# Reading the moving activations of a two-block transformer kernel from the last column to the first

## What is computed

```python
proj = rmsnorm(h, norm1_w) @ w_in
h = h + mixed @ w_out
z = rmsnorm(h, norm2_w) @ mlp_w1
h = h + jnp.square(jax.nn.relu(z)) @ mlp_w2
...
proj = x @ w_in_2
merged = g_a * (o_a @ w_o_dsa) + g_b * (o_b @ w_o_moba)
y = merged @ w_out_2
y = (jax.nn.silu(g) * u) @ w_ffn_out
```

## Time and profile before

| | before |
|---|---|
| median of 3 runs | 2574.3 us |
| span of the profiled execution | 2573.8 us |
| PE busy | 2555.9 us (99%), 15948 matmuls |
| PEld busy (loads of the stationary side) | 2297.6 us (89%) |
| DVE busy | 1572.9 us (61%) |
| ACT busy | 1189.7 us (46%) |
| POOL busy | 27.9 us (1%) |
| HBM read, rate over the span | 464.93 MB, 181 GB/s |

### The profile page before, as it was taken

The page is one execution under the profiler, slowest core; times in us unless marked ns, Lnnn a source line. Parts: engine busy times, 40 slices in busy tenths (PEclk is TensorE's granted clock), DMA queues, the critical chain, the costliest instruction groups (busy, mean ns, idle before and its releaser), DMA issues.

```text
span 2573.8 us, 41371 instructions
## 1 busy us (share of the span) xinstructions
PE 2555.9 (99%) x15948; PEld 2297.6 (89%) x15948; DVE 1572.9 (61%) x2178; ACT 1189.7 (46%) x1609; POOL 27.9 (1%) x70
## 2 busy tenths in 40 slices
PE   9999999999999999999999999999999999999998
PEld 7999988888888888899999999988999888888886
DVE  5444856556556555565565566666876776656665
ACT  5543545434444344544444454444544445445442
POOL 1000000000000000000000000000000000000000
PEclk9999999999999999999999999999999999999999
DMA  7664556666555665574455565565576577567753
GB/s 251 179 180 130 165 181 180 196 196 186 190 184 191 196 195 186 173 224 154 131 165 170 160 200 183 186 213 161 150 205 180 189 196 191 189 186 186 195 196 114
DMA packets 467782, 468.80 MB, mean 182 GB/s; under 512 B 9246, under 2 KB 384142, under 8 KB 466862
## 3 DMA queue, kind: packets, MB, share of 16 engines
q1 hardware_dynamic: 465600, 459.31, 58.5%
q0 software_dynamic: 2064, 7.82, 0.9%
HBM read 464.93 MB, written 2.10 MB: 181 GB/s over the span
## 4 chain that ended last, share of the span: by engine, by line
PE 97%; DVE 1%; ACT 1%; DMA 0%; issue 0%; SPq 0%; DVEq 0%; ACTq 0%
PE ps L693 17%; PE ps L696 11%; PE ps L697 11%; PE ps L698 11%; PE ps L725 11%; PE ps L727 11%; PE ps L726 11%; PE ps L694 9%; PE ps L789 1%; DMA region<-in_mem 0%; PE ps L1130 0%; PE ps L1101 0%; DVE w_lo L2091 0%; PE ps L1137 0%; PE ps L1173 0%; PE ps L1006 0%
## 5 line engine op out<-in xcount | busy, mean ns | idle before, releaser
L2091 DVE TENSOR_TENSOR w_lo<-raw,w_hi 128x1024 fp32r<-128x1024 f32 (+1 forms) x867 | 1047.5, 1219 | 766.0 <-ACT w_hi L1438 764.5
L1438 ACT ACTIVATE w_hi<-raw 128x1024 fp32r<-128x1024 f32 (+1 forms) x869 | 902.1, 1051 | 909.4 <-PE ps L727 410.1
L693 PE MATMUL ps<-xa,w_hi 128*128 128x512 f32 x1920 | 666.0, 391 | 0.0
L696 PE MATMUL ps<-xa,w_hi 128*128 128x256 f32 (+2 forms) x2112 | 607.4, 288 | 0.0
L698 PE MATMUL ps<-xa,w_lo 128*128 128x256 f32 (+2 forms) x2112 | 595.0, 282 | 0.0
L697 PE MATMUL ps<-xa,w_hi 128*128 128x256 f32 (+2 forms) x2112 | 593.4, 281 | 0.0
L694 PE MATMUL ps<-xa,w_lo 128*128 128x256 f32 x1920 | 537.3, 280 | 0.0
L693 PEld LDWEIGHTS ps<-xa,w_hi 128*128 128x128 f32 x1920 | 360.1, 188 | 79.6
L697 PEld LDWEIGHTS ps<-xa,w_hi 128*128 128x128 f32 x2112 | 398.4, 189 | 2.0 <-issue 1.0
L696 PEld LDWEIGHTS ps<-xa,w_hi 128*128 128x128 f32 x2112 | 397.2, 188 | 3.2 <-issue 2.0
L698 PEld LDWEIGHTS ps<-xa,w_lo 128*128 128x128 f32 x2112 | 396.5, 188 | 0.0
(11 more groups left out here) (364 smaller groups left out, 2537.0 us busy)
## 6 DMA issues: line engine op xcount, KB each, us to landing
raw<-in_mlp_w SPq DMA_DIRECT2D x128, 1024.0 KB
raw<-in_w_in SPq DMA_DIRECT2D x106, 1024.0 KB
raw<-in_w_ffn_in SPq DMA_DIRECT2D x176, 512.0 KB
raw<-in_w_ffn_out SPq DMA_DIRECT2D x44, 1024.0 KB
raw<-in_w_out SPq DMA_DIRECT2D x32, 1024.0 KB
raw<-in_w_o_dsa SPq DMA_DIRECT2D x8, 1024.0 KB
raw<-in_w_o_moba SPq DMA_DIRECT2D x8, 1024.0 KB
raw<-in_w_kv_mem SPq DMA_DIRECT2D x7, 1024.0 KB
```

The costliest lines, as they stand in the source:

```text
L693: nc.tensor.matmul(o, hi, x.rearrange("p a n -> p (a n)"), start=opens and ci == 0, stop=False)
L696: nc.tensor.matmul(o, hi, x_hi, start=opens and ci == 0, stop=False)
L1438: return nc.scalar.activation(dst, src, ACT.Copy, **kw)
L2091: V.tensor_tensor(w_lo[:, ps_ % CUT, 0:n], raw[:, bs % RAW, n * half:n * half + n], w_hi[:, ps_ % CUT, 0:n].bitcast(F32), ALU.subtract).th ...
```

## The change

In `pair` alone, the moving operand and the piece of the bank that is written are both given with their last dimension turned round, so that the last token's column is read first and its sum is written first, at the column where it stood before. The stationary operand is as before, and so are all values and all places. `broad_piece`, where weights move, is not touched, nor are the attention steps. No instruction is added, removed or moved, on any engine: the same matmuls stand in the same order, with the same waits, only with a step of -1 in place of 1 in two of their three operands. With the new function ahead of it, every line of the kernel after is 4 higher than before.

```diff
+            def down(v):
+
+                return v[:, ::-1]
+
...
                                 if wide:
 
-                                    nc.tensor.matmul(o, hi, x.rearrange("p a n -> p (a n)"), start=opens and ci == 0, stop=False)
-                                    ins = nc.tensor.matmul(o[:, 0:SEQ], lo, x_hi, start=False, stop=closes and ci == 3)
+                                    nc.tensor.matmul(down(o), hi, down(x.rearrange("p a n -> p (a n)")), start=opens and ci == 0, stop=False)
+                                    ins = nc.tensor.matmul(down(o[:, 0:SEQ]), lo, down(x_hi), start=False, stop=closes and ci == 3)
                                     continue
-                                nc.tensor.matmul(o, hi, x_hi, start=opens and ci == 0, stop=False)
-                                nc.tensor.matmul(o, hi, x_lo, start=False, stop=False)
-                                ins = nc.tensor.matmul(o, lo, x_hi, start=False, stop=closes and ci == 3)
+                                nc.tensor.matmul(down(o), hi, down(x_hi), start=opens and ci == 0, stop=False)
+                                nc.tensor.matmul(down(o), hi, down(x_lo), start=False, stop=False)
+                                ins = nc.tensor.matmul(down(o), lo, down(x_hi), start=False, stop=closes and ci == 3)
```

## The result

The kernel after takes 2596.52 us (median of 3 runs, 2596.43 to 2596.7) against 2574.3 us before: ratio 1.0084, 95% interval 1.0066 to 1.0102. It is slower by 22 us. The profiled executions have spans of 2595.0 and 2573.8 us, 21.2 us apart. My forecast was no difference; the case that came is the small loss C.

The account below looks back on a forecast made before the run. TensorE, busy 2555.9 of 2573.8 us, was taken as the bound, so time is a sum over matmuls. The change's terms were all 0: 2573.8 + 0, plus 0.5 us from profiled span to median, gives 2574.3 us; range 2505 to 2637.

Parts of the forecast that it names:

- the small loss C: In `pair`, the turned stream starts at a worse offset: half of 5.6 ns gives 2606 us, all 2637; chance 0.26.
- What bounds the kernel: Whole kernel: TensorE busy 2555.9 of 2573.8 us, so time is a sum over matmul start-to-start distances.
- 11328 matmuls, half a ns decides: In `pair`, 11328 of 15948 matmuls are touched; one ns each is 11.3 us, half a ns decides the sign.
- The write side costs 0: In `pair`, writing the bank with a step of -1 adds no time, against the skill's PSUM line rule.
- the order in the bank: In `pair`, the bank is whole at handover and same-column writes lie at least 256 columns apart; cost 0.
- I take 0: In `pair`, reading with a step of -1, bounded by 1431 us loss and 111 us gain, was put at 0.
- the 5.6 ns of the "mv" phase: "mv" against MLP down projection, 232.9 against 227.3 ns: stationary offset differs; up to 63 us on 11328 matmuls.
- the moving side is less touchy than the stationary one: Argument against C: narrow maps on `xb` and `xo`, at other offsets, have means within the same 281 to 287 ns.
- Rival D, the gain: In `pair`, the turned stream meets stationary loads less often: half of 111 us gives 2519 us, far end 2463; chance 0.30.
- Half pace (B): In `pair`, step -1 loses the pairing of neighbours on read or write: 2573.8 + 1431 = 4005 us; chance 0.12.
- a change without effect (E): In `pair`, the turned patterns on both sides are made ascending again: 2574 us; chance 0.02.

Follow-up runs that it names:

- the four offsets: Change (turned reads and writes) with activations beginning 28, 32, 36 or 40 floats into their buffer (EVEN), other buffers in place: 2590.95, 2592.81, 2596.52, 2583.22 us.
- EVEN = 40: Activations beginning 40 floats into their buffer in place of 36: 2571.91 us ascending (kernel before otherwise), 2583.22 us turned (the change otherwise).

## Why the prediction was wrong

**What bounds the kernel.** Right. The time is a sum over matmul distances. The 21.2 us between the spans are the sum of the changed distances, no wait came in, and the other engines have the busy time of before.

**11328 matmuls, half a ns decides.** Right, and it is what made "0" a weak choice: the mean change is 1.9 ns, four times the bound.

**The write side costs 0.** Right, by the run that turns the write alone (0.9997), and with it the order in the bank.

**"I take 0" for the read with a step of -1.** This is the step that failed: the term for the turned read, put at nothing. The runs showed 1.9 ns on each touched matmul in its place, 21.2 us between the traces, and 22.5 us for the kernel that turns the read alone (2597.97 us). My argument was that a stream that takes its columns one by one has no reason in the rows to mind the sign. But I had written down the reason to doubt it just before: the 5.6 ns of the "mv" phase suggest that distances hang on where the operands lie, and a turned read changes where the stream begins for every touched matmul. (Start to start it is 4.9 ns, 233.2 against 228.3; my 227.3 came from a window's count, which is too low.) A row that shows that a place is sensitive, together with a change of that place in all matmuls, makes exact equality the least likely outcome, and the choice was between a loss and a gain. I put the middle of -5.6 and +5.6 as the likeliest value as if the case had been a scatter around it. My range, 2505 to 2637 us, holds the time, but it was made wide enough for a gain or a loss, so that says nothing for the forecast.

**Rival C, the small loss.** It was right in sign and in place, the read. That the turned read only starts at a worse offset, its mechanism, isn't shown: none of the four offsets heals it. Its size was half of 5.6 ns on all, 32 us, and 63 at the most; measured are 6.67 ns on a wide pair, 1.3 to 3.3 on gate maps, 2.2 on those of 258 columns and -0.55 on `xb` and `xo`, 21.2 us together. What I held against it, that the moving side is less touchy than the stationary one, was wrong: 16 bytes of the moving side's offset took the gate maps from 113.34 to 120.00 ns.

**Rival D, the gain.** It didn't come for the kernel as a whole. It isn't nonsense either: at EVEN = 40 the gate maps are 0.9 ns faster turned than ascending. Half pace (B) is ruled out by the 1.9 ns, and a change without effect (E) by the run with the turned read alone.

**What stays open.** Why each form, offset and direction has the distance that it has. Halving the loads together with the rows written takes 3 ns from ascending gate maps, the stream's own address moves the wide pairs where a shift of the weights didn't, and stretches carry something on; no run isolates what a turned stream meets. The traces give a hint for a next test. The distances repeat in a fixed order: in the MLP's up projection of the kernel before 226, 117, 236, 121, 227, 113 ns, over three pairs, and after the change some 238 and 116 ns in every pair. Work of other engines that comes at irregular times would hardly do that; it wasn't tested.

## What to carry to other kernels

Where matmuls stand back to back, the start address of the moving side is worth a sweep in steps of 16 bytes, stage by stage. In this kernel it was worth up to 18 us of 2574, nearly as much as the change, and the best place differs between matmuls of 512 and of 256 columns. A descending write cost nothing here, and a descending read was far from half pace; but the read changes which offsets are good, so tune the two together and expect no neutral outcome. And keep all other buffers in place while doing so: when `xa` grew so that the buffers behind it moved by 32 bytes, maps on `xb` and `xo` went from 118.3 to 120.0 ns. A measurement over one stretch of a stage can mislead as well: the same gate maps, turned and with half loads, have 119.9 ns in one part and 117.8 in the next.

## What was not expected of the hardware

- A map can have several steady distances at the same addresses: 226.67 and 228.33 ns in the MLP's down projection, by the stage ahead of it, and 118.7 and 116.7 ns in the gate maps within one run.
- The two directions of a bank write can't be told apart (2574.37 against 2575.49 us), while a read turned the same way costs 22 us.
- With loads of 64 columns in place of 128 (and 64 rows written in place of 128), the ascending gate maps come from 116.67 to 113.33 ns, though the stream is the same 256 columns. Turned ones run at 117.8 in a part of the stage and at 119.9, as with whole loads, in another.
